# Two-layer hybrid encoder on one core: five seven-product couples in a group's first wide pair, four in its second, and their sums placed and ordered anew

## The reference, cut to what matters

```
x = x + RMSNorm(mixed)
f = square(relu(rms_norm(x, g_ffn_pre) @ w_up)) @ w_down     # w_up 2048 x 8192, w_down 8192 x 2048
x = x + rms_norm(f, g_ffn_post)
```

## Time and profile before

| | |
|---|---|
| time, median of 3 runs | 1889.78 us (1889.22 to 1890.29) |
| the profiled execution | 1889.38 us, its span in the trace 1887.3 us |
| TensorE busy | 1874.9 us, 99% of the span, granted clock 0.999 |
| VectorE busy | 1497.9 us, 79% |
| ScalarE busy | 1111.4 us, 59% |
| DMA | 390.92 MB, mean 207 GB/s |

### The profile page before, as it was taken

How to read it: one execution, slowest core, us unless ns; L and a number is a source line. 1 busy time by engine, 2 the same in 40 slices (tenths; PEclk the granted TensorE clock), 3 DMA queues, 4 the chain that set the end, 5 groups by cost and what they waited for, 6 DMA issues and landing times.

```text
span 1887.3 us, 27369 instructions
## 1 busy us (share of the span) xinstructions
PE 1874.9 (99%) x9950; PEld 1672.1 (89%) x9950; DVE 1497.9 (79%) x1885; ACT 1111.4 (59%) x1485; POOL 118.5 (6%) x166
## 2 busy tenths in 40 slices
PE   9999999999999999999999999999999999999998
PEld 7988988988988998898888888889889889989987
DVE  6886657898699689788877757678977996897886
ACT  6455656855665565566554556568556655645662
POOL 3920010000000000000000000100000000000000
PEclk9999999999999999999999999999999999999999
DMA  8665366757566666767576554586676666567673
GB/s 290 201 221 181 112 201 226 236 182 255 189 198 216 214 198 195 236 202 241 210 234 225 187 168 134 170 275 194 197 236 207 195 212 221 183 207 235 221 257 124
DMA packets 170068, 390.92 MB, mean 207 GB/s; under 512 B 12161, under 2 KB 14321, under 8 KB 168433
## 3 DMA queue, kind: packets, MB, share of 16 engines
q1 hardware_dynamic: 167904, 377.58, 61.8%
q10 hardware_dynamic: 2064, 12.08, 1.7%
HBM read 382.53 MB, written 7.08 MB: 206 GB/s over the span
## 4 chain that ended last, share of the span: by engine, by line
PE 95%; DVE 3%; issue 1%; ACT 0%; DMA 0%; POOL 0%; DVEq 0%; POOLq 0%; ACTq 0%
PE acc_pair L573 25%; PE acc_pair L578 13%; PE acc_pair L539 8%; PE acc_pair L540 8%; PE acc_pair L541 8%; PE acc_pair L874 7%; PE acc_pair L873 7%; PE acc_pair L872 7%; DVE w_lo L1445 1%; PE t_bank L874 1%; PE t_bank L873 1%; PE t_bank L872 1%; PE o_bank L791 1%; DVE h_both L1501 1%; PE ssa_bank L872 1%
## 5 line engine op out<-in xcount | busy, mean ns | idle before, releaser
L995 ACT CAST w_hi<-raw 128x1024 fp32r<-128x1024 f32 x687 | 703.6, 1048 | 476.4 <-DVE raw L1998 190.7
L1445 DVE TENSOR_TENSOR w_lo<-raw,w_hi 128x1024 fp32r<-128x1024 f32 x687 | 827.4, 1232 | 169.0 <-ACT w_hi L995 161.8
L573 PE MATMUL acc_pair<-h_both,w_hi 128*128 128x512 f32 x2176 | 560.3, 380 | 0.2
L573 PEld LDWEIGHTS acc_pair<-h_both,w_hi 128*128 128x128 f32 x2176 | 371.4, 190 | 30.4 <-issue 0.5
L578 PEld LDWEIGHTS acc_pair<-h_both,w_lo 128*128 128x128 f32 x2176 | 327.4, 190 | 29.2
L578 PE MATMUL acc_pair<-h_both,w_lo 128*128 128x256 f32 x2176 | 330.5, 274 | 0.0
L872 PE MATMUL acc_pair<-w_hi,f_hi 128*128 128x512 f32 x504 | 191.0, 379 | 0.0
L873 PE MATMUL acc_pair<-w_lo,f_hi 128*128 128x512 f32 x504 | 191.0, 379 | 0.0
L874 PE MATMUL acc_pair<-w_hi,f_lo 128*128 128x512 f32 x504 | 191.0, 379 | 0.0
L539 PE MATMUL acc_pair<-w_hi,h_both 128*128 128x512 f32 x444 | 170.4, 384 | 1.8 <-DVE w_lo L1445 1.6
L540 PE MATMUL acc_pair<-w_lo,h_both 128*128 128x512 f32 x444 | 168.3, 379 | 0.0
(11 more groups left out here) (252 smaller groups left out, 2293.8 us busy)
## 6 DMA issues: line engine op xcount, KB each, us to landing
raw<-in_w_up SPq DMA_DIRECT2D x256, 512.0 KB, 4.4
raw<-in_w_down SPq DMA_DIRECT2D x240, 512.0 KB, 5.0
raw<-in_w_in SPq DMA_DIRECT2D x128, 512.0 KB, 4.7
raw<-in_w_out SPq DMA_DIRECT2D x64, 512.0 KB, 5.3
raw_side<-in_w_down SPq DMA_DIRECT2D x16, 512.0 KB, 7.0
x_kept<-x ACTq DMA_DIRECT2D x4, 1024.0 KB, 6.2
x<-x_kept ACTq DMA_DIRECT2D x4, 1024.0 KB, 6.1
x<-in_x SPq DMA_DIRECT2D x8, 256.0 KB, 7.5
```

The lines of the kernel that those rows point to most:

```text
L573: pe.matmul(acc_pair[b][:, m, :], w_hi[:, slot, col:col + P], x_both.rearrange("p s (a n) -> p s n a", a=2), start=(slot, k) == (0, 0), st ...
L995: act.copy(w_hi[:, half * PAIRS + p, :], raw[:, p, :]).then_inc(hi_made, 1)
L1445: dve.tensor_tensor(w_lo[:, slot, :], src[:, p, :], w_hi[:, slot, :].bitcast(F32), ALU.subtract).then_inc(lo_made, 1)
```

## The change

1. **Couples.** The first pair of a group has couples at slots 0, 4, 6, 10, 12, the second at 0, 4, 8, 12: 32 in a layer instead of 28. The order of k-tiles follows from it.
2. **Activation sums** for the five couples are taken from both halves of units 0 and 1 and from the first half of unit 2 (before: both halves of units 1 and 2, the last cast falling into unit 3); in group 0 the first two come from `t_bank`.
3. **Weight sums** have another form: the third first, in a function of its own (`weight_third`, both raw slots needed), then one 512-wide sum and one 1024-wide difference. The 1024-wide one has a broadcast operand. The `o_bank` and `t_bank` products change places.
4. **Slots 6 and 7** are made after the last up unit, behind couple 1's `sums_lo` and the new couple's weight sums.
5. **ScalarE to VectorE**: relu and square of the last unit's second half are one VectorE instruction (`last_square`). **VectorE to ScalarE**: the shared sums of groups 0 and 1 (`first_shared`, four copies) and group 0's first `wide_sums` (`first_sums`).
6. **Shared sums** of groups 2 and 3 are one VectorE instruction, 128x2048.
7. **At a group's end** the four `wide_sums` of the second pair, before behind the next unit's first four slots, are spread: slot 0, two sums, slot 1, two sums, slots 2 and 3.

```
-SEVEN_AT = (0, PAIRS, RING, RING + PAIRS)
-SEVEN_UNIT = ((1, 0), (1, 1), (2, 0), (2, 1))
+SEVEN_AT = ((0, 4, 6, 10, 12), (0, 4, 8, 12))
+SEVEN_UNIT = ((0, 0), (0, 1), (1, 0), (1, 1), (2, 0))[:max(COUPLES)]
...
# ScalarE
+                def first_shared(g):
+                    if g == 0:
+                        act.wait_ge(x_saved, 16 * T * (l + 1))
+                    act.wait_ge(t_used, 3 * seven_no(l, g, 0, COUPLES[0]) - 1)
+                    for k in range(SHARED):
+                        act.copy(kept_sums[:, 1 - pair_at(g, 0), k, :], shared[:, k, :]
+                                 ).then_inc(shared_free, 1)
...
+                    last_unit(g)
+                    wide_hi(g, 0, 6)
                     if not last:
+                        wide_hi(g, 1, 0, 2)
+                        if g < T:
+                            first_shared(g)
+                        two_hi(g, 1, 2)
+                        if first:
+                            first_sums()
+                        wide_hi(g, 1, 4)
...
# VectorE
+                def last_square(g):
+                    z = act_f[:, 1, :]
+                    dve.wait_ge(acc_free[1], 1 + a0 + ACC_F + g * 8 + CHUNKS)
+                    dve.scalar_tensor_tensor(z, z, 0.0, z, ALU.max, ALU.mult
+                                             ).then_inc(f_ready, 1)
...
+                def weight_third(g, q, n):
+                    i = SEVEN_AT[q][n]
+                    hu = hu0 + HU_F + g * HU_GROUP + 2 * CHUNKS + PAIR_HALVES * q + i // PAIRS
+                    top_r, low_r = (raw[:, i % PAIRS + m, c_cols(1)] for m in range(2))
+                    for m in range(2):
+                        dve.wait_ge(raw_loaded[i % PAIRS + m], hu * 16 + 16)
+                    dve.tensor_tensor(top_r, low_r, top_r, ALU.subtract).then_inc(t_third, 1)
...
+                    dve.wait_ge(t_third, no + 1)
+                    dve.tensor_tensor(out[:, 0, :], top[:, c_cols(1)], top[:, c_cols(0)], ALU.add
                                       ).then_inc(t_step, 1)
...
+                    dve.wait_ge(t_step, 2 * no + 1)
...
+                    dve.tensor_tensor(out[:, 1:3, :], low, out[:, 0:1, :].to_broadcast([P, 2, CH]),
+                                      ALU.subtract).then_inc(t_step, 1)
...
+                def couple_lo(g, q, i):
+                    n = SEVEN_AT[q].index(i)
+                    weight_sums(g, q, n)
+                    two_lo(g, q, i)
+                    if i + 2 in SEVEN_AT[q]:
+                        weight_third(g, q, n + 1)
+                    sums_lo(g, q, n)
+                def wide_lo(g, q, begin):
+                    for i in range(begin, SLOTS, 2):
+                        if i not in SEVEN_AT[q]:
+                            two_lo(g, q, i)
+                            continue
+                        if i - 2 not in SEVEN_AT[q]:
+                            weight_third(g, q, SEVEN_AT[q].index(i))
+                        couple_lo(g, q, i)
...
                 def wide_pair(g, q, first, last=False):
-                    seven_lo(g, q, 2, hu + 2, 0)
-                    seven_lo(g, q, 3, hu + 3, 1)
+                    wide_lo(g, q, (6, 4)[q])
                     if q == 0 and not last:
-                        weight_sums(g, 1, 0, nxt)
-                        split_lo(nxt, 0, (0, 1))
-                        sums_lo(g, 1, 0)
-                        shared_sums(g)
-                        split_lo(nxt, 0, (2, 3))
-                        wide_sums(g, q, first)
-                        seven_lo(g, 1, 1, nxt + 1, 1)
+                        weight_third(g, 1, 0)
+                        couple_lo(g, 1, 0)
+                        if g >= T:
+                            shared_sums(g)
+                        two_lo(g, 1, 2)
+                        if not first:
+                            wide_sums(g, q)
...
                     else:
-                        split_lo(nxt, 0)
-                        wide_sums(g, q, first)
+                        split_lo(nxt, 0, (0,))
+                        wide_sums(g, q, (0,))
+                        split_lo(nxt, 0, (1,))
+                        wide_sums(g, q, (1,))
+                        split_lo(nxt, 0, (2, 3))
                         split_lo(nxt + 1, 1)
...
                     def last_unit():
-                        seven_lo(g, 0, 0, nxt, 0)
-                        s_rest(g, 3)
+                        weight_third(g, 0, 0)
+                        couple_lo(g, 0, 0)
+                        two_lo(g, 0, 2)
...
+                        weight_third(g, 0, 1)
+                        weight_sums(g, 0, 1)
                         f_stands(g, u, 0)
                         turned_lo(g, u, 0)
-                        split_lo(nxt + 1, 1, (0, 1))
+                        two_lo(g, 0, 4)
                         turned_sum(g, u, 1)
-                        split_lo(nxt + 1, 1, (2, 3))
-                        f_stands(g, u, 1)
+                        last_square(g)
+                        if 6 in SEVEN_AT[0]:
+                            weight_third(g, 0, 2)
                         turned_lo(g, u, 1)
                         sums_lo(g, 0, 1)
```

More of the change, by code:

```diff
@@ L137, with k_order, t_buffer @@
 WIDE_LAYER = 2 * FF_GROUPS - 1
-SEVEN_AT = (0, PAIRS, RING, RING + PAIRS)
-SEVEN_UNIT = ((1, 0), (1, 1), (2, 0), (2, 1))
-K_ORDER = (4, 5, 0, 1, 6, 7, 2, 3, 8, 9, 12, 13, 10, 11, 14, 15)
-SHARED = 4
+SEVEN_AT = ((0, 4, 6, 10, 12), (0, 4, 8, 12))
+COUPLES = tuple(len(at) for at in SEVEN_AT)
+LAYER_COUPLES = FF_GROUPS * COUPLES[0] + (FF_GROUPS - 1) * COUPLES[1]
+SEVEN_UNIT = ((0, 0), (0, 1), (1, 0), (1, 1), (2, 0))[:max(COUPLES)]
+PLAIN_LAST = tuple(SLOTS - 2 not in at for at in SEVEN_AT)
+SHARED = 4
+def k_order(q):
+    pairs = [4 * u + 2 * b for u, b in SEVEN_UNIT[:COUPLES[q]]]
+    plain, order = iter([k for k in range(0, KT, 2) if k not in pairs]), []
+    for i in range(0, SLOTS, 2):
+        k = pairs[SEVEN_AT[q].index(i)] if i in SEVEN_AT[q] else next(plain)
+        order += [k, k + 1]
+    return order
+K_ORDER = (k_order(0), k_order(1))
+def t_buffer(q, n):
+    return (q * COUPLES[0] + n) % 2
 def pair_at(g, q):
@@ L166, in wide_done, with relu_no @@
 def wide_done(l, g, q):
-    return l * WIDE_LAYER + g * 2 + q + 1
+    group = PLAIN_LAST[0] + PLAIN_LAST[1]
+    layer = FF_GROUPS * PLAIN_LAST[0] + (FF_GROUPS - 1) * PLAIN_LAST[1]
+    return l * layer + g * group + sum(PLAIN_LAST[:q + 1])
+def relu_no(l, g, u, b):
+    return l * (7 * FF_GROUPS - 2) + g * 7 + u * 2 + b - 2
 def trunc_bits(v, bits):
@@ L912, in seven @@
                         bank_free(0, 0, q, result)
-                    three(acc_pair[0][:, 0, :], f_hi[:, k1, early], f_lo[:, k1, early],
-                          w_hi[:, s1, left], w_lo[:, s1, left], first, False)
+                    mm = three(acc_pair[0][:, 0, :], f_hi[:, k1, early], f_lo[:, k1, early],
+                               w_hi[:, s1, left], w_lo[:, s1, left], first, closing)
+                    if closing:
+                        mm.then_inc(acc_done, 2)
                     if first:
@@ new lines, in wide_hi @@
+                def wide_hi(g, q, begin, end=SLOTS):
+                    for i in range(begin, end, 2):
+                        two_hi(g, q, i)
+                        if i in SEVEN_AT[q]:
+                            sums_hi(g, q, SEVEN_AT[q].index(i))
+                def first_shared(g):
[5 more added lines that the diff above has]
+                                 ).then_inc(shared_free, 1)
@@ L1943, in narrow_sum, with wide_sums @@
                                   hu0 + HU_F + g * HU_GROUP + 2 * CHUNKS + c * 2 + 1)
-                    down_sum(g, c, t, False, acc_bank[t])
-                def wide_sums(g, q, first):
+                    down_sum(g, c, t, acc_bank[t])
+                def wide_sums(g, q, which=range(T)):
                     result = a0 + ACC_F + g * 8 + CHUNKS + 2 * q
                     hu = hu0 + HU_F + g * HU_GROUP + 2 * CHUNKS + PAIR_HALVES * q
-                    for t in range(T):
+                    for t in which:
+                        if g == 0:
+                            dve.wait_ge(rstd_ready, T + l * RS_LAYER + RS_X2 + T)
+                        else:
+                            dve.wait_ge(acc_free[t], 1 + a0 + ACC_F + 2 * CHUNKS)
@@ L1964, in s_sums @@
                     out = s_sum[n]
-                    dve.tensor_tensor(out[:, 0, :], z[:, 0, h_cols(1)], z[:, 1, h_cols(1)], ALU.add
+                    if g + u == 0:
+                        early = [t_bank[0][:, h_cols(2 * b + k)] for k in range(2)]
+                        late = [out[:, 0, :], t_bank[1][:, h_cols(2 * b + 1)]]
+                        dve.tensor_copy(late[0], t_bank[1][:, h_cols(2 * b)]).then_inc(late_kept, 1)
+                        dve.wait_ge(late_kept, 2 * l + n + 1)
@@ L2038, in combine @@
+                def shared_sums(g):
+                    dve.wait_ge(t_used, 3 * seven_no(l, g, 0, COUPLES[0]) - 1)
```

(7 more changed lines are left out.)

241 lines of the change are left out of this document (118 added, 123 removed).

## The result

The kernel after takes 1925.06 us (median of 4 runs, 1923.73 to 1927.83); the kernel before, run beside it, 1889.97. The ratio is 1.0188, 95% interval 1.0171 to 1.0206: 35.1 us slower, where 23.6 were forecast. The profiled execution of after took 1927.83 us with a span of 1925.7, the highest of its runs; against the span of before, 1887.3, it stands at +38.4.

What follows compares the result with a forecast made beforehand. The number of TensorE matmuls was taken as the bound, with VectorE 91% busy in wide pairs. Second-pair waits 12.69, spread sums 1.95, less 0.25 and 2.59, gave +11.80 us a layer, +23.6 in all: 1913.0 us, range 1895 to 1919.

Steps and rivals of the forecast that it cites:

- Couple and matmul prices, what is removed: TensorE: 0.216 us a matmul, 38.20 a five-couple pair; four products fewer a layer save 2.59 us, 5.2 in all.
- VectorE through a first pair: Group's first pair: fifth couple, longer load waits and `last_square` use up VectorE's 5.2 us lead; `t_lo` ends 39.87, pair 38.20.
- the load wait of slot 10: First pair: VectorE idles 1.16 us ahead of slot 10's third, which needs both loads (5.1 us against 3.94 of work).
- The margin that the forecast found at slot 12: First pair: slot 12's `w_lo` stands at 28.3 us, TensorE wants it at 28.5, just enough.
- Waits at the second pair's start: TensorE waits for late VectorE or ScalarE work: groups 0 to 3 1.30, 2.83, 4.48, 4.08 (narrow unit), 12.69 us a layer.
- the sum: Whole kernel: 12.69 + 1.95 - 0.25 - 2.59 = +11.80 us a layer, +23.6 for two, 1913.0 us.
- Costed at nothing: `s_sums` of group 0's first two couples (about 3 us, in VectorE's idle time) and `first_sums` on ScalarE: no cost.
- The spread sums: Group's end: slot 2's `w_lo` late, TensorE waits 0.65 us three times a layer, 1.95; old order's 0.25 late start goes.
- Rival 4: Loads take 5.4 us; second-pair couple step of 10.25 exceeds TensorE's 9.73; about +3.5 a layer, 1920 us; chance 0.08.
- Rival 1: Wide pairs: loads land within 3.94 us of VectorE work; +4.4 a layer, 1898.2 us; chance 0.17, including anything up to the forecast.
- Rivals 2 and 3: 2: 1024-wide difference takes 0.6 us, 1887.6 us, chance 0.07; 3: VectorE's lead lasts through the pair, 1884.2 us, chance 0.08.

## Why the prediction was off

The direction and the mechanism were right, the size was not: +35.1 us against +23.6, above the range's end of 1919.

- **Couple and matmul prices, what is removed**: right. 24 matmuls fewer, and the first pair of group 0, where nothing is waited for, takes 38.21 us (38.20).
- **VectorE through a first pair**: right to 0.3 us at each point that the trace shows, the load wait of slot 10 (1.29 us idle against 1.16) among them. The margin that the forecast found at slot 12, 0.2 us, was smaller than that: TensorE waited there up to 1.14 us.
- **Waits at the second pair's start**: right in place and releaser. Group 0, 0.99 us (1.30 forecast); group 1, 1.32 and 1.15 (1.30 and 1.38); group 2, 3.60 (3.95 and 0.38 behind it, which did not come); group 3, 3.05 and before it 0.84 at slot 12 (4.08 in one place). The listed waits of the two layers are 26.4 us without the first group's, where the steps had 29.3. The steps count from where the next matmul would have started, the list from 0.16 us later; with that for each of these 19 waits the trace has 29.5. So the waits themselves were right in sum. That it is so close is luck: the second pairs came out lower and slot 12 higher.
- **The step that failed is the sum**, in that it put each wait down at its length. At each of the four waits of 3 us and more TensorE fell to half clock, which cost 8.8 us in the profiled run. The kernel before holds no wait of this size, so no row of it showed the price, and I didn't bound it. The run with nothing but added waits shows it: 26.2 us of waits made 37.0. Against the forecast's +23.6 the profiled pair of executions stands 14.8 us higher: 8.8 half clock, 1.6 the first group, about 2 the late second matmul behind each wait, 1.1 ahead of the feed-forward parts, 1.3 not assigned.
- **Costed at nothing**: wrong in layer 1, right in layer 2. The rows made in group 0 delayed ScalarE's cast, its DMA issues stood behind the cast, and the `w_hi` casts behind those: 1.40 us of TensorE's time, 1.6 with the 0.16. With the cast moved behind the issues the wait fell to 0.45 and to none (four and five couples with the old weight sums).
- **The spread sums**: a wait of 0.6 at six units for 0.65, right. But the old order that they were compared with was priced by the kernel before, where VectorE is early. In the kernel after it costs 12 us more.
- **Rival 4** had the loop and put it at loads of 5.4 us. With my own 5.1 it is 2.58 + 2.27 + 5.1 = 9.95, already over TensorE's 9.73; measured it is 10.20. I charged it to the rival alone. In the kernel after the unit starts show little of it: with the spread order TensorE waits 0.6 us there, with the old one 1.0 to 2.2.
- **Rival 1** (hidden loads, 1898.2) describes the run with half loads, which gave 1905.2. The landing of 512 KB, 4.8 us in the new profile, kept it from being so here.
- **Rivals 2 and 3**: neither came. The 1024-wide difference took 1.14 us (743.98 to 745.12), and in group 2 `t_lo` was handed over 1.4 us behind the first pair's end.

**What stays open.** Of the 8 us that four couples still cost, the weight sum order and the spread order together are 6 (1898.3 to 1892.2 without both); the remaining 2.1 were not divided further. The 1.3 us of the account without a place were not looked for.

## What to carry to other kernels

When a change lets the busiest engine wait where it never waited, price the wait by its length and by what the clock does behind it; in the run with added waits, 26.2 us of them cost 10.8 us on top, 9.5 of it half clock at those of 3.4 us and more. An operation that reads two loads at once belongs behind one that reads the first alone: count the loop from freeing a buffer to the next load's landing, and compare its length, not the engine's busy share, with the pace of the engine that it feeds. And an order of work is only good or bad for the engine that is late under it: the same spread order cost about 3 us with VectorE early and saved 12 with VectorE late.

## What the runs showed of the hardware

TensorE's granted clock behind a wait, over the profiled executions of all kernels of this study: none of the 31 waits between 1.3 and 2.0 us was followed by half clock, two of the seven between 2.03 and 2.34 us were, and 20 of the 21 from 2.49 us on, the 3.74 above being the exception. What followed was half clock for 3.4 us, 6.8 us or, at the wait of 8.42, 10.2 us, and not in proportion to the wait: 3.4 at 4.72 us, 6.8 at 3.05. It began between 4.3 us ahead of the wait's end and 1.3 us behind it, and only what lies behind the end costs time. So waits of 3.0 to 4.2 us cost from nothing (3.74) to 3.1 us (4.13) on top of their length, by half of what lies behind the end.

Part of the spread between executions of one kernel goes with the clock. The four executions of the kernel after, 1927.83, 1923.73, 1925.98 and 1924.14 us, had mean granted clocks of 0.994, 0.996, 0.994 and 0.995; a mean higher by 0.002 is 7.7 us less at half clock in a span of 1925.7, and so 3.9 us less time, as an estimate. It is not all of the spread: of four couples with the old order, three executions had 0.996 and took 1908.32, 1910.00 and 1914.43 us.
